# Stick-breaking attention in a hybrid block: the next scores go ahead of the value product on TensorE

## The reference, cut to what matters

```python
for q0 in range(0, seqlen, 128):                       # blocks of 128 queries
    z = einsum("bqhd,bkhd->bhqk", qb, kb) * 64 ** -0.5
    strict = s_pos < t_pos
    log_keep = where(strict, log_sigmoid(-z), 0.0)
    after = cumsum(log_keep, axis=3, reverse=True) - log_keep
    weights = where(strict, exp(log_sigmoid(z) + after), 0.0)
    out = einsum("bhqk,bkhd->bqhd", weights, vb)
```

## Time and profile before

| | us |
|---|---|
| median of 3 runs (2594.44 to 2597.7) | 2595.68 |
| the profiled execution's own time | 2594.92 |
| its span, first to last instruction | 2593.2 |
| projections and scan, up to the first scores | 1296.4 |
| attention, 1296.36 to 2222.17 | 925.8 |
| output product, from there | 371.0 |

### The profile page before, as it was taken

The page is one execution under the profiler, slowest core; times in us unless marked ns, Lnnn a source line. Parts: engine busy times, 40 slices in busy tenths (PEclk is TensorE's granted clock), DMA queues, the critical chain, the costliest instruction groups (busy, mean ns, idle before and its releaser), DMA issues. The chain is left out here.

```text
span 2593.2 us, 40310 instructions
## 1 busy us (share of the span) xinstructions
PE 2519.7 (97%) x13783; PEld 1777.6 (69%) x13783; DVE 1671.6 (64%) x2077; ACT 1352.9 (52%) x2116; POOL 1575.4 (61%) x1391
## 2 busy tenths in 40 slices
PE   5999999999999999989999999999999999999998
PEld 3888777777888888866655555555555555688887
DVE  7332556646213565267788889898888989765553
ACT  5343333345333333344477888787788878522221
POOL 4666666687777777658866667676676767200000
PEclk8999999999999999999989999999999999999999
DMA  3543323333433333256741221212122121433330
GB/s 116 166 146 120 119 104 119 111 102 128 145 114 118 126 130 118 94 138 179 199 132 50 66 86 39 90 46 79 57 66 83 42 90 55 150 99 96 95 99 33
DMA packets 204245, 268.75 MB, mean 104 GB/s; under 512 B 13456, under 2 KB 137680, under 8 KB 197408
## 3 DMA queue, kind: packets, MB, share of 16 engines
q1 hardware_dynamic: 203632, 266.04, 32.2%
q10 hardware_dynamic: 432, 0.39, 0.0%
HBM read 169.36 MB, written 97.03 MB: 103 GB/s over the span
## 5 line engine op out<-in xcount | busy, mean ns | idle before, releaser
L2119 POOL TENSOR_TENSOR a_w<-a_beta,a_rest 128x1024 f32<-128x1024 f32 (+2 forms) x320 | 560.3, 1751 | 268.0 <-DVE a_rest L2067 149.6
L804 POOL TENSOR_TENSOR f_l_lo<-f_wst,f_l_hi 128x512 fp32r<-128x512 f32 x312 | 406.6, 1306 | 295.9 <-ACT f_l_hi L667 295.7
L2067 DVE TENSOR_TENSOR_SCAN a_rest<-a_keep,a_rest,a_floor 128x513 f32<-128x513 f32 x384 | 468.5, 1262 | 10.7 <-ACT a_keep L2021 10.7
L1968 PE MATMUL a_turn<-a_ident,a_w 128*128 128x128 f32 (+1 forms) x2432 | 348.5, 282 | 8.9 <-DVE a_wt L2005 5.9
L1968 PEld LDWEIGHTS a_turn<-a_ident,a_w 128*128 128x128 f32 (+1 forms) x2432 | 256.8, 140 | 118.0 <-issue 92.2
L533 PE MATMUL f_xz<-f_t_hi,f_l_hi 128*128 128x512 f32 x832 | 329.3, 396 | 0.0
L533 PE MATMUL f_xz<-f_t_hi,f_l_lo 128*128 128x512 f32 x832 | 325.3, 391 | 0.0
L533 PE MATMUL f_xz<-f_t_lo,f_l_hi 128*128 128x512 f32 x832 | 325.2, 391 | 0.0
L2005 ACT COPY a_wt<-a_turn 128x512 f32<-128x512 f32 (+3 forms) x456 | 233.1, 531 | 170.5 <-PE a_turn L1968 168.9
L2021 ACT ACTIVATE a_keep<-a_z 128x1024 f32<-128x1024 f32 (+4 forms) x352 | 300.6, 854 | 3.3 <-PE a_z L1950 3.2
L2021 ACT ACTIVATE a_beta<-a_z 128x1024 f32<-128x1024 f32 (+4 forms) x352 | 300.8, 855 | 1.5 <-POOL a_w L2133 1.3
(11 more groups left out here) (307 smaller groups left out, 4369.1 us busy)
## 6 DMA issues: line engine op xcount, KB each, us to landing
f_wst<-in_w_pairs SPq DMA_DIRECT2D x52, 1024.0 KB, 5.9
scratch_gate<-outs SPq DMA_DIRECT2D x64, 256.0 KB, 2.5
o_g<-scratch_mixed SPq DMA_DIRECT2D x32, 512.0 KB, 5.5
outs<-in_x SPq DMA_DIRECT2D x20, 512.0 KB, 4.5
scratch_xbc<-outs SPq DMA_DIRECT2D x36, 256.0 KB, 2.1
scratch_q_hi<-outs SPq DMA_DIRECT2D x32, 256.0 KB, 3.2
scratch_q_lo<-outs SPq DMA_DIRECT2D x32, 256.0 KB, 3.7
scratch_v<-outs SPq DMA_DIRECT2D x32, 256.0 KB, 2.3
```

What stands on the lines that cost most here:

```text
L804: return nc.gpsimd.tensor_tensor(out, a, b, op).then_inc(done, 1)
L1968: mm = nc.tensor.transpose(turn[h][0:rows, qi * P:(qi + 1) * P], tile[:, h, x:x + rows], ident[:, :])
L2067: mm = nc.vector.tensor_tensor_scan(rest[r % RS][:, h, tn - 1::-1], top, low, start, ALU.mult, ALU.max)
L2119: done = nc.gpsimd.tensor_tensor(tile[:, :, 0:tn], beta[r % KEEPS][:, :, 0:tn], rest[r % RS][:, :, 1:tn + 1], ALU.mult)
```

## The change

In each step of TensorE's loop the scores of two steps ahead are issued right behind the transposes, and the application of the block in front comes last. Nothing is added or removed, no tile, wait, semaphore or line of another engine is changed.

```diff
             for n in range(-2, N + LAG + 1):
                 if 0 <= n - LAG < N:
                     turn_block(n - LAG)
+                if 0 <= n + 2 < N:
+                    scores(n + 2)
                 if 0 <= n - LAG - 1 < N:
                     apply(n - LAG - 1)
-                if 0 <= n + 2 < N:
-                    scores(n + 2)
```

## The result

| | before | after |
|---|---|---|
| median, 6 runs each | 2595.07 us | 2605.19 us |
| lowest and highest | 2593.57, 2597.7 | 2601.84, 2606.31 |
| profiled execution, its span | 2594.92, 2593.2 | 2606.03, 2604.3 |
| attention stage in the profile | 925.81 | 933.77 |

The ratio is 1.0036, with a 95% interval of 1.0025 to 1.0046: slower by 6.5 to 11.9 us. The forecast was 2604 us, 8.2 us more.

The account below looks back on a forecast made before the run. TensorE, with hardly an idle moment in the attention, was taken as the bound. Five terms of 1.04 us a pair in sum gave about 8.2 us over eight pairs, so 2604 us (+0.32%), range 2598 to 2612.

Parts of the forecast that it names:

- TensorE sets the end, and ACT is never short of scores: Attention stage: PE has hardly an idle moment; ACT waits for scores only 4 times, 3.2 us, so earlier scores buy nothing.
- The work costs the same: Full PE step: transposes, `apply` and scores take 2.92 us in either order; the unseen border is worth 0.
- The border rival: Scores to `apply`: the load of `apply` is hidden there, up to 68 us less, 2536 to 2570 us; chance 0.07.
- Waits for `beta` at eight positions: Scores of a pair: `beta` ends too late, waits 0.13, 0.16, 0.78, 0.52, up to 0.16, and 0.37 us.
- the rival: PE's waits for `beta` add up, nothing swallowed: 2.12 us a pair, 17 us, time 2613 us; chance 0.13.
- What the stands swallow: Transposes standing for DVE's copy take up waits at 13, 24 to 26 and 38 to 43; 0.11 us left at the last.
- DVE's delay by the gate product: `gated` starts later behind the later `apply`: 0.18 us at position 12, 0.10 each at 21 and 34.
- The shortened step for the narrow scores: Position 12: the narrow scores take 0.48 us, estimated from half of a full one's 0.88.
- The sum: Attention stage: 1.04 us lost a pair, 8.3 us for eight, about 8.2 us after first and last pair exceptions.
- the signs named in advance: Profile after: full step still 2.92 us, idles moved to scores at 13 and 16, attention about 8 us longer, other stages unchanged.
- 0.9 us is small beside them: SyncE transfers: the third chunk's queries, up to 0.9 us later, have four steps of up to 2.92 us to arrive.

Follow-up runs that it names:

- e1: The first experiment: changed kernel, but old order at positions 4, 11, 13, 16, 24, 25, 38, 40; 2597.48 us, ratio 1.0008 to the kernel before.
- e2: Kernel before, with the new order only at positions 4, 11, 13, 16, 24, 25, 38, 40; 2602.8 us, ratio 1.0026 to before.
- e6: Changed kernel with head 1's copies of blocks 6, 18 and 35 moved from DVE to ACT; 2601.86 us, ratio 1.0023 to the kernel before.

## Why the prediction was right

**TensorE sets the end, and ACT is never short of scores.** Right. No pair gains anything but the first in its opening; ACT still waits for scores 4 times, 2.8 us after against the 3.2 of the earlier trace rows.

**The work costs the same.** Right, the full step is 2.92 us in both orders. The border rival is excluded by the weight loads of the profile after and by the first experiment, where 36 swapped steps cost 2 us together. Five borders seen in before (three of the old order, one each from the stage's first and last steps) had been enough to guess the sixth.

**Waits for `beta` at eight positions.** Right in place, and in size at 4, 11, 13 and 16. At 24 and 25 they were 0.25 us together where the forecast had up to 0.16, and at 38 and 40 0.49 where it had 0.37, up to 0.1 more (both with the stands taken away); the stands hid the difference. Their sum, 2.12 us a pair by the earlier trace rows, is not what is lost, and this was the point at which the forecast was decided: adding them up gives 17 us. That is about the cost that the swap has when DVE's stands are taken away (18.2), so the rival was a true description of another kernel.

**What the stands swallow.** Right: at 13 the whole wait vanishes (0.16 us for the stage when swapped alone), at 38 to 43 most of it: 0.15 us a pair is left where the forecast had 0.11.

**DVE's delay by the gate product.** Right at 21 and 34, about 0.1 us each, as the transposes behind 26 and 43 show with those steps swapped alone. At 12 nearly all of the 0.18 us is the wait of position 11 passed on, as the forecast's sum has it: swapped alone, that step costs 0.03 to 0.05. The shortened step for the narrow scores, an estimate of 0.48 us, measured 1789.35 - 1788.87 = 0.48.

**Sizes.** The sum was 8.2 and the stage took 8.0 more. That it is so close is in part luck: a pair lost 1.09 us in place of 1.04, about 8.5 in all, and the 0.6 us of the first pair's opening, which nobody forecast, took that back. The median moved by 10.1, within its own interval of 6.5 to 11.9; the 2 us between are not explained by a step and are of the size by which executions differ. Of the signs named in advance, that the other stages stay unchanged did not hold to better than the 3.4 us by which the part ahead of the scores differs between executions.

**A sentence that was too easy.** "0.9 us is small beside them", of the transfers. The load of the third chunk's queries is in time with little to spare in the sixth pair: it held the scores in four of the nine profiles, for 0.19 us in before, 0.31 in e2, 0.99 in e6 and 1.08 in e1. In the profile after it held nothing; it landed 0.37 us before it was needed. So it does not touch the profiled result. Whether it adds to some of the runs that were not profiled is not shown.

## What to carry to other kernels

When an engine works through a written order and two neighbouring pieces can be swapped, ask of each which event it waits for and how early that event is: the piece whose input is long there should stand in front of the one whose input is just coming, as it fills the hole for nothing. Get the slack from the timeline at each position of the period, not from the mean; here 36 of 44 steps cost 2 us together, and one position made half of the loss. Do not add waits up: between two waits on the same engine look for a later stand on another engine, because it swallows the first as long as its own releaser is not delayed; and where such stands exist, they are what is worth removing (here 12.7 us in the stage by moving three copies).

## What the runs showed of the hardware that was not expected

A change of shape between groups of matmuls was never bridged by an early weight load, whichever two shapes met: the load unit sat free for 0.81 us at `apply` to scores, 0.35 at scores to `apply`, 0.17 at transposes to scores. At each of the about 1,045 borders of every trace the next load began no more than 0.07 us before the modelled end of the last matmul. The semaphore wait at each border is not the reason: the first transpose of head 1 waits for a semaphore too, with no change of shape, and where that wait is met its load runs ahead like the others (at 1803.43 in before, 0.27 us before the modelled end of the matmul in front). The Trainium skill ("TensorEngine Tiling (Array Packing)", Key Properties) says that changing the tiling mode drains TensorE, and all borders of these traces agree.

The same small transfer (8 KB of values, behind 1 MB of them) held SyncE for very different times at the same place of the program, ahead of the sixth pair's queries: 3.65 us in before and 4.81 in e1, and 2.85 to 4.89 over the nine profiles.

```profile
1886.46 3.65 SPq L1732 DMA_DIRECT2D o_values<-scratch_v  x1
```

```profile
1888.12 4.81 SPq L1732 DMA_DIRECT2D o_values<-scratch_v  x1
```

The queries' issue stands behind it, and the scores had to wait in just the four profiles where it took 3.65 us or more. Why it differs is not shown. The new order adds to the risk in two ways. `gated`, and with it the whole chain of issues, comes later: against the transposes of position 12 it starts 0.74 us later in after and 0.89 later in e1 than in before, about what the forecast allowed. And where the scores of position 12 go ahead of `apply`, they want the queries 0.4 us sooner.
